# A second block problem in the last gate/up group of two feed-forward networks

## What is computed

```python
def swiglu(x, w_gate, w_up, w_down):            # w_gate, w_up: 2048 x 5632; w_down: 5632 x 2048
    return (jax.nn.silu(x @ w_gate) * (x @ w_up)) @ w_down

x = x + 0.5 * swiglu(rms_norm(x, ffn1_norm[l]), ffn1_w_gate[l], ffn1_w_up[l], ffn1_w_down[l])
...
x = x + 0.5 * swiglu(rms_norm(x, ffn2_norm[l]), ffn2_w_gate[l], ffn2_w_up[l], ffn2_w_down[l])
```

## Time and profile before

| | us |
|---|---|
| median of 3 executions | 1760.78 (1760.40 to 1761.28) |
| profiled execution, its own time | 1760.41 |
| its span, first to last instruction | 1758.6 |
| TensorE (PE) busy | 1747.8 |
| VectorE (DVE) busy | 1521.5 |
| ScalarE (ACT) busy | 1055.9 |
| GpSimd (POOL) busy | 297.7 |

### The profile page before, as it was taken

The page is one execution under the profiler, slowest core; times in us unless marked ns, Lnnn a source line. Parts: engine busy times, 40 slices in busy tenths (PEclk is TensorE's granted clock), DMA queues, the critical chain, the costliest instruction groups (busy, mean ns, idle before and its releaser), DMA issues.

```text
span 1758.6 us, 21446 instructions
## 1 busy us (share of the span) xinstructions
PE 1747.8 (99%) x7791; PEld 1440.0 (82%) x7791; DVE 1521.5 (87%) x1760; ACT 1055.9 (60%) x1262; POOL 297.7 (17%) x581
## 2 busy tenths in 40 slices
PE   9999999999999999999999999999999999999998
PEld 7888888888888888888888888888888888888886
DVE  7799999999887786777878888899999999887786
ACT  7566666666555554555555456566666666555544
POOL 0102111111112112111121131121111111210001
PEclk9999999999999999999999999999999999999999
DMA  7756666666676667657555667666666666676654
GB/s 268 239 204 213 206 216 221 228 221 214 206 238 216 213 193 239 204 170 223 191 183 169 212 216 253 221 209 205 218 224 227 222 219 214 210 252 208 221 191 133
DMA packets 201802, 374.92 MB, mean 213 GB/s; under 512 B 19808, under 2 KB 20448, under 8 KB 201696
## 3 DMA queue, kind: packets, MB, share of 16 engines
q1 hardware_dynamic: 182992, 351.97, 59.8%
q0 software_dynamic: 18272, 21.01, 4.1%
q10 hardware_dynamic: 432, 0.56, 0.1%
HBM read 351.44 MB, written 4.19 MB: 202 GB/s over the span
## 4 chain that ended last, share of the span: by engine, by line
PE 99%; DMA 0%; SPq 0%; ACT 0%; DVE 0%; issue 0%; DVEq 0%; ACTq 0%
PE bank L905 17%; PE bank L907 17%; PE bank L908 17%; PE bank L922 10%; PE bank L923 10%; PE bank L924 10%; PE bank L1043 4%; PE bank L1046 4%; PE bank L1045 4%; PE bank L887 1%; PE bank L888 1%; PE bank L889 1%; DMA x<-in_x_dram 0%; PE bank L1231 0%; PE bank L1248 0%; PE bank L1104 0%
## 5 line engine op out<-in xcount | busy, mean ns | idle before, releaser
L1326 ACT ACTIVATE w_hi<-raw 128x1024 fp32r<-128x1024 f32 x443 | 467.3, 1058 | 309.8 <-PE bank L908 199.1
L1787 DVE TENSOR_TENSOR w_lo<-raw,w_hi 128x1024 fp32r<-128x1024 f32 x443 | 540.1, 1224 | 127.9 <-ACT w_hi L1326 123.0
L2647 POOL DMA_DIRECT2D turn_in<-gate x448 | 219.1, 497 | 837.0 <-DVE gate L1897 762.1
L905 PE MATMUL bank<-w_hi,xT_hi 128*128 128x512 f32 x812 | 318.1, 392 | 0.0
L907 PE MATMUL bank<-w_lo,xT_hi 128*128 128x512 f32 x812 | 316.1, 389 | 0.0
L908 PE MATMUL bank<-w_hi,xT_lo 128*128 128x512 f32 x812 | 316.1, 389 | 0.0
L905 PE MATMUL bank<-w_hi,hT_hi 128*128 128x512 f32 x528 | 205.4, 389 | 0.0
L907 PE MATMUL bank<-w_lo,hT_hi 128*128 128x512 f32 x528 | 205.4, 389 | 0.0
L908 PE MATMUL bank<-w_hi,hT_lo 128*128 128x512 f32 x528 | 205.4, 389 | 0.0
L1340 ACT ACTIVATE w_hi<-first_b 128x1024 fp32r<-128x1024 f32 x140 | 148.7, 1062 | 90.7 <-PE bank L908 38.2
L1340 ACT ACTIVATE w_hi<-second_b 128x1024 fp32r<-128x1024 f32 x129 | 136.9, 1061 | 104.7 <-DVE second_b L2064 47.3
(11 more groups left out here) (259 smaller groups left out, 2884.0 us busy)
## 6 DMA issues: line engine op xcount, KB each, us to landing
raw<-in_ffn_w_down_dram SPq DMA_DIRECT2D x132, 512.0 KB, 4.8
raw<-in_ffn_w_up_dram SPq DMA_DIRECT2D x102, 512.0 KB, 6.3
raw<-in_ffn_w_gate_dram SPq DMA_DIRECT2D x101, 512.0 KB, 5.8
raw<-in_w_in_dram SPq DMA_DIRECT2D x80, 512.0 KB, 4.3
first_b<-in_ffn_w_gate_dram SPq DMA_DIRECT2D x40, 512.0 KB, 4.1
first_b<-in_ffn_w_up_dram SPq DMA_DIRECT2D x40, 512.0 KB, 4.5
second_b<-in_ffn_w_gate_dram SPq DMA_DIRECT2D x34, 512.0 KB, 5.3
second_b<-in_ffn_w_up_dram SPq DMA_DIRECT2D x34, 512.0 KB, 5.4
```

Of the source, the lines that this page charges most:

```text
L905: pe.matmul(acc, hi[:, kt, ts], w_hi[slot][:, kk], start=(opens and kk == 0), stop=False, skip_group_check=problems(ffn, c) > 0)
L1326: act.activation(w_hi[f % RING][:], raw[m % RING][:], ACT.Copy).then_inc(hi_ready, 1)
L1787: dve.tensor_tensor(w_lo[f % RING][:], src[:], w_hi[f % RING][:].bitcast(F32), ALU.subtract)\
L2647: pool.dma_start(to[32 * j:32 * j + 32, q].rearrange("r k t i -> r (k t i)"), mid[32 * q:32 * q + 32, j].rearrange("r k t i -> r (k t i)") ...
```

## The change

Group 10 has two problems instead of one in both networks, so group 9 becomes a (2,2) stage and group 10 a (2,1) stage with four gate and four up chunks. The first block of its second problem is loaded into kept_down, since the old place is where the ninth hidden block lies. That block is split later (behind P2 of group 10 on ScalarE, behind G1 and the fourth sum on VectorE, there with a wait for P7' on TensorE). The tenth block is split behind U3 on ScalarE and behind P6 on VectorE. In the (2,1) stage the order of forms goes from "U0 P1 P5 U1 P3 P6 U2 P7 U3" to "U0 P1 U1 P5 U2 P3 P6 U3 P7"; FIRST's token sum, which stood behind G5 of a group 10 with six gate chunks, stands behind U0, its low part behind P5. The loads of FIRST's blocks wait for the second problem of group 10 instead of that of group 9, as they share their space.

```diff
-PROBLEMS = ((0, 1, 2, 2, 2, 2, 2, 2, 2, 2, 1, 1, 2), (0, 2, 2, 2, 2, 2, 2, 2, 2, 2, 1, 1, 2))
+PROBLEMS = ((0, 1, 2, 2, 2, 2, 2, 2, 2, 2, 2, 1, 2), (0, 2, 2, 2, 2, 2, 2, 2, 2, 2, 2, 1, 2))
...
-CHAIN_AFTER = {(2, 2): (0, 0, 0, 0, 1, 1, 1, 1, 2, 2), (2, 1): (0, 0, 1, 1, 2), (1, 1): (0, 1, 2, 3, 4),
+CHAIN_AFTER = {(2, 2): (0, 0, 0, 0, 1, 1, 1, 1, 2, 2), (2, 1): (0, 1, 2, 2, 3), (1, 1): (0, 1, 2, 3, 4),
...
         def blocks(c):
+            if c == FIRST - 1:
+                return (first_b11, kept_down), (first_b12, second_b12), (first_b22, second_b22)
             if c < FIRST:
...
                     if c == FIRST:
-                        sp.wait_ge(lo_ready, ch + AT[ffn, c - 2, P4, 1] + 1)
-                        sp.wait_ge(chunk_used, ch + AT[ffn, c - 2, P7, 1] + 1)
+                        sp.wait_ge(chunk_used, ch + AT[ffn, c - 1, P7, 1] + 1)
+                        if p == P4:
+                            sp.wait_ge(lo_ready, ch + AT[ffn, c - 1, P4, 1] + 1)
...
-                    if c == GROUPS - 1 and at == (1, P1, 0):
+                    if c == GROUPS - 1 and at == (0, U, 1):
                         split_tokens(FIRST, 0, token_use(ffn, FIRST, 0) + 1)
...
-                        if at == (0, U, 2):
+                        if at == ((1, P2, 0) if c == GROUPS - 2 else (0, U, 2)):
                             split_hidden(hid_of(ffn), c - 1)
...
+                        if at == (0, U, 3):
+                            split_hidden(hid_of(ffn), c - 1)
                         if at == (1, P7, 0):
                             keep_up_upper()
+                        if at == (1, G, 0):
+                            open_gate_lower()
                         if at == (1, P2, 0):
-                            split_hidden(hid_of(ffn), c - 1)
-                            open_gate_lower()
-                        if at == (1, G, 2):
                             gated(0)
+                        if at == (1, G, 1):
                             gated(1)
...
-                    if c == GROUPS - 1 and at == (0, G, 5):
+                    if c == GROUPS - 1 and at == (0, U, 0):
                         token_blocks(FIRST, 0, ch, ffn)
                         token_sum(FIRST, 0, token_use(ffn, FIRST, 0))
-                    if c == GROUPS - 1 and at == (0, U, 1):
+                    if c == GROUPS - 1 and at == (1, P5, 0):
                         split_tokens(FIRST, 0, token_use(ffn, FIRST, 0))
...
-                            if at == (0, U, 3):
+                            if at == (0, U, 3) and c < GROUPS - 2:
                                 split_hidden(hid, c - 1)
                         else:
+                            if at == (0, G, 3):
+                                turn_lower()
                             if at == (1, P1, 0):
                                 first_sum(0)
-                                turn_lower()
                             if at == (1, P3, 0):
                                 second_sum(0)
+                            if at == (1, P6, 0):
                                 third_sum(0)
-                            if at == (1, P2, 0):
                                 split_hidden(hid, c - 1)
...
                             fourth_sum(nx, 0)
+                            if c == GROUPS - 2:
+                                dve.wait_ge(chunk_used, ch + AT[ffn, nx, P7, 1] + 1)
+                                split_hidden(hid, c - 1)
```

## The result

| | before | after |
|---|---|---|
| median, us | 1760.72 of 6 (1760.40 to 1761.28) | 1769.26 of 6 (1767.08 to 1771.22) |
| ratio | | 1.0049, interval 1.0039 to 1.0060 |
| profiled execution, its span | 1760.41, 1758.6 | 1767.08, 1765.3 |

The change makes the kernel 8.5 us slower, where 5.5 were forecast; the median lies 0.3 us beyond the upper end of the range. Two things catch the eye. The six executions after spread over 4.1 us, those before over 0.9. And the profiled execution is the fastest of the six, so it shows 6.7 us of the 8.5; the other 1.8 to 2.2 us have to be found elsewhere.

The account below looks back on a forecast made before the run. TensorE, busy 99%, bounds the kernel: only fewer matmuls or new waits move the end. Laid out on one clock, gains and delays net +2.73 us a network, 5.5 in all: 1766.2 us (+0.31%), range 1762.4 to 1769.0.

Parts of the forecast that it names:

- The gain: TensorE, group 10: six fewer matmuls save 1.36 us a network, less 0.13 inherited by group 9: 1.23 us.
- Step 1: ScalarE, ninth block's high part behind hi(P2): snapshot ends at 397.89, so group 10's G0 starts 0.37 us late.
- Step 2: VectorE up to low(U0): steps start 1.13 to 1.14 us apart; low(G3) comes 0.73 later, still in time.
- Step 3: VectorE, token sum (3.04 us) now behind low(U0): U1 starts 0.68 us late, including the 0.37 at G0.
- Step 4: VectorE, low(U3) behind third sum and tenth block's low part: U3 loses 2.22 us a network, floor 1.3.
- VectorE without idle from the gate product to U3: Sign expected in both networks' profiles, beside the gaps before U1, U3 and the downs' G0.
- Step 5: Tail "U3 P7 G0": the downs' G0 waits for P7's snapshot, 0.94 us lost, bounds 0.8 to 1.1.
- Step 6: Loads: U1's, third of a burst, in time by 0.3 us at the median; price nothing or up to 1.6.
- rival (c): Loads before U1: the burst's third load lands last, +1.6 us a network, 1769.4 us; chance 0.11.
- Rival (d): TensorE behind U3's gap: clock falls, 18 matmuls at 1.2 GHz cost 4.08 us a network, 1774.3; chance 0.04.
- Rival (b): Group 10: the order has its cover, only the six matmuls' gain stays, 1758.3 us; chance 0.05.
- Rival (a): VectorE less full: delays up to U1 hidden, U3 at its 1.3 floor, +1.0 us a network, 1762.8; chance 0.22.

Follow-up runs that it names:

- z1: y2 without the four small steps of the downs' first token sum (output not the reference's); 1760.84 us, 1760.08 before.
- x2: Changed kernel with VectorE's low part of the tenth block moved behind low(G0) of the downs; 1765.31 us, 1760.38 before.
- x3: Kernel before with P7 moved behind U5, straight before the downs' G0; 1762.37 us, 1760.38 before.
- y3: x2 with TensorE's wait for the last snapshot moved from in front of the downs' G0 to its middle; 1765.14 us, 1760.67 before.
- x1: Changed kernel with the loads of U1 and U2 issued ahead of the downs' two block loads in group 10; 1767.04 us, 1760.38 before.
- y1: The changed kernel, unaltered, run once more; 1768.99 us, 1760.67 before.
- z3: z2 without the four small steps of the first token sum (output not the reference's); 1759.25 us, 1760.08 before.
- y2: Changed kernel with the edits of x1 and x2 together; 1763.39 us, 1760.67 before.
- y4: Changed kernel with x1, x2 and y3's edits, third sum behind low(U3), ninth block's high part back behind hi(U2); 1762.55 us, 1760.67 before.
- z2: y4 with the downs' G0 waiting for the hidden blocks up to the ninth only; 1761.29 us, 1760.08 before.
- x5: Changed kernel with the downs' first token sum made by GpSimd instead of VectorE; 1778.04 us, 1760.38 before.
- w: Kernel before with VectorE repeating low(U3) of group 10 ahead of the real one, so TensorE waits there; 1765.15 us, 1760.08 before.

## Why the prediction was right and wrong

**The sign and the kind were right.** Six matmuls a network went, TensorE's gaps took their place, and each lies where it was put, with the releaser named. Step by step:

- **The gain** (1.23 us a network): 7779 matmuls for 7791, and no other change in TensorE's rate between the gaps.
- **Step 1**: snapshot forecast for 438.25 on the trace's clock (397.30 + 40.95), found at 438.23; 0.38 us for 0.37.
- **Step 2**: low(U0) forecast for 451.88, found at 451.84. VectorE's steps from group 9's U3 on came out within 0.04 us in sum, so steps of 1.22 us do start 1.14 us apart, and the 1.1 us a network that an empty pipe between them would have added did not come. The Trainium skill, "VectorE: DVE Perf Modes", section "The DRAIN you can't avoid", adds to the rule that the prediction took from it that a next operation which is not held starts earlier. The prediction left that out; the rows agree with it.
- **Step 3**: U1, 0.72 late in all with G0's, for 0.68. z1 shows that the token sum is its cause: without 1.67 us of it, it is gone.
- **Step 4, U3**: 2.13 for 2.22, and x2 shows the tenth block's low part as 1.28 of it. The sign "VectorE without idle from the gate product to U3" failed: it idled 0.67 before low(P5) and 1.13 before low(P6). The second was in the working (second sum, then hi(P6), then low(P6)) and not in the sign; the first is the miss below.
- **Step 5**: 0.97 for 0.94, and x3 gives 0.96 to 1.0 for it alone. Nothing was late behind it, as was counted; y3 shows how near the next is: two low parts became late once the snapshot was 0.5 us out of the way.

**Step 6 failed, in one half of its reasoning.** The landing was forecast between 414.0 and 417.9, which is 454.95 to 458.85 in the trace, and hi(U1) was found waiting until 457.23: in the range, 0.3 us later than the median put it (416.0, or 456.95; the load took 6.6 us for 6.4), and as needed (416.29 + 40.95 = 457.24). That it met the need to the hundredth is luck. The price "nothing, if in time" was wrong all the same. I asked only whether TensorE's U1 would wait. Behind hi(U1) on ScalarE stood two more steps, the token sum's high part and hi(P5), and hi(P5) was due 0.7 us before it went (458.45 for 459.15). P5 (0.30) and P6 (0.39 over the forecast) lost 0.7 us a network, 1.4 in all. x1 took the load out of the way and got the forecast's own sum. That is rival (c)'s transfer at a price inside its bounds, at other places than rival (c) had it (U1's gap stayed as forecast).

**Rival (d) came true at 0.4 of its price**: the clock fell in some executions behind U3's gap, for about 8 matmuls and not 18: 1.6 us a fall and not 4.08. It most likely brought the last 1.8 to 2.2 us of the median and most of the width of 4 us: y1's profile has two falls, 3.2 of its 3.7 us over the profile of after, but no execution near the median was profiled. I gave it 0.04, because no row before showed a low clock amid matmuls; but no row before had a gap of 2 us either, so that was silence and no evidence. The range had no room for (c) and (d) at once, each small, and the median lies beyond it.

**Rival (b)** (the gain alone, 1758.3) is what z3 comes near to, and only by leaving work out. **Rival (a)** (U3 at its floor of 1.3) did not come: even with the load in time (x1) U3 lost 2.13. VectorE was not free ahead of it.

**What the experiments say of the change.** In the stretch of after from the token sum to U3 (columns as in the earlier trace rows) VectorE is busy 17.02 of 19.1 us:

```profile
452.90:472.00 19.10, 17.02 (x72) 12.83 (x70) 17.02 (x19) 11.29 (x13) 7.12 (x15) 1.00 0.75 230
```

With none of its gaps TensorE would take 3.3 us less for this stretch (U1, P5, P6 and U3 together), some 15.8, and VectorE's steps alone need 17, of which the token sum is 3.03. Both order and amount count. The order of y2 (x1 and x2 together) brought the 3.3 us down to 1.2, which is what VectorE's time exceeds TensorE's by. Another order still (y4, z2) only moved most of that to P7, and with work taken off VectorE (z1, z3) all but 0.1 us of it went. Two more losses lie outside this stretch, 0.38 us at G0 and 0.97 at the tail; with TensorE's wait placed inside G0 (z2, z3) 0.63 stayed of both. By the medians every complete version tried is still 1.2 us or more above the kernel before.

## What to carry to other kernels

Fewer matmuls gain only where the engines that feed them have room in that very stage; add up the feeding engine's steps for the stage. A new order can win back only the waits beyond what these steps exceed TensorE's time by; the rest moves to another form. When a load is "just in time" for one step, ask for every step that stands behind it on the same engine, since each of them is late by what the wait exceeds its own room. And an idle gap of TensorE is to be priced at its length plus its restart, and a gap as long as those here (1.75 to 1.85 us idle) also with what a fallen clock costs in some executions; since a profile shows one execution, take a second one where the times spread wider than before.

## What was not expected of the hardware

- Idle gaps of 1.75 to 1.85 us (2.0 to 2.1 us lost) halved TensorE's granted clock in six of the ten networks profiled with such a gap (y1 and x5 both, x1 and w one, after none), 0 to 6 matmuls behind the gap and for about 8 matmuls: 1.6 us each time. No profile whose losses stay at or under 1.4 us (x2, x3, y2, y3, y4, z1, z2, z3) shows it there. The spread of the times is a hint and no proof: z3, with no such gap, still had two of eleven executions 1.9 to 2.5 us above its median, and these were not profiled.
- A fp32 sum on GpSimd, 128 x 1024 in 3.47 us (2.40 in the second network), stretched VectorE's step beside it from 1.22 to some 3.4 us in both; with 3.03 us of work a network moved off VectorE the kernel took 9 us more than after.
- U1's load, third of a burst, landed 6.6 us after its issue in after, where ScalarE had waited 4.7 us for it, and 7.0 us after its issue in y3's second network (ScalarE waited 5.8 us), with the same order on the queue.
